# One down product moved ahead of an up product, and TensorE's expert loop turned by half a block

## The chip, the cores and the metric

The kernel runs on one core of a Trainium2 chip. TensorE multiplies, VectorE (DVE), ScalarE (ACT) and GpSimd (POOL) do the elementwise work and the indirect transfers, and SyncE (SP) issues the weight loads. The metric is the device time of one execution in microseconds (us). Times of trace rows are counted from the first instruction of the span.

## The reference, cut to what matters

One transformer block: attention, a residual, and then a mixture of experts. For each of 512 tokens a router picks 4 of 32 experts. Each expert is

```python
hu   = xb @ w1[e] + b1[e]                # "up": 1024 -> 2048
gate, lin = hu[:, :1024], hu[:, 1024:]
gate = min(gate, 7); lin = clip(lin, -7, 7)
act  = gate * sigmoid(1.702 * gate) * (lin + 1)
y    = act @ w2[e] + b2[e]               # "down": 1024 -> 1024
```

and the results, weighted by the gates, are added to the token's row. A final normalization follows. All weights are float32: 8 MB of w1 and 4 MB of w2 for each expert.

## The kernel before

The first part (attention, output projection, router, the tables of the routing) is not touched. The change is in the last part, which runs over blocks. A block is 32 tokens of one expert; an expert has as many blocks as its tokens need, and with this input there are 81 blocks (`nb`), numbered from 0. Experts stand in an order of places; place 0 has blocks 0, 1, 2, place 1 has blocks 3 and 4, place 2 starts with block 5.

**Weights.** The arena holds two experts, one for even places (`par` 0) and one for odd ones (`par` 1). SP loads one place after the other, w1 in four transfers of 2048 KB (L508) and w2 in two (L513), all on one queue. Quarter c of a new w1 waits on `w1_read`, until the first block of the place between has read its own quarter c; w2 waits until the last block that uses the old w2 has read it (`w2_read`, `y_done`).

**A block's work.** POOL gathers its token rows (`gather`, L600). DVE turns them into `xT` (`turn_rows`, L1255), the one buffer of its kind. TensorE does the up product into PSUM (`up`, L1816, 64 matmuls, and 4 for the bias, L1826). DVE and ACT make the activation (`hidden`, L1308 to L1314; `sigmoid`, L849), DVE turns it into `actT` (`turn_hidden`, L1301), also one buffer, and TensorE does the down product (`down`, L1854, 64 matmuls, 4 for the bias, L1846). DVE and ACT scale the result, and POOL adds it to the tokens' rows in memory (`scatter`, L609). A small product, `slot_product` (L1786), makes the list of tokens of a block some places ahead.

**Both places in code.** Which half of the arena a block reads is known only at run time. `up_of` (L1833) and `down_of` (L1862) are therefore an If and an Else, each with the whole product in it. `places_of` (L1802) loads a word of a table from SBUF into a register, and splits it into the places of two blocks.

**TensorE's order.** The first blocks are written out, the rest is a loop with two blocks to a pass. Before the change the order is

```
up0 up1 up2 down0 down1 up3 | slot5 down2 up4 | slot6 down3 up5 || slot7 down4 up6 | slot8 down5 up7 || ...
```

where `|` stands for the start of a block of the loop (test of `g < nb` or `g + 1 < nb`, L1894 and L1896, and the load of `places_of`) and `||` for the turn of the loop (L1892) as well. After the last block the loop runs on, with empty passes, up to its fixed count.

**DVE's order** in the written-out part is: rows of block 1 are turned inside `hidden(0)`, rows of block 2 inside `hidden(1)`, and so on, since `xT` is free only once the up product of the block before has ended.

Of the kernel before, what the change touches and what calls it, by code (L numbers as in the profile page):

```python
# [44 lines left out]
AHEAD = 64  # L45
MAXBLK = (T * TOPK + NE * (SLOTS - 1)) // SLOTS
NG = MAXBLK + 7
# [86 lines left out]
def build(nc, I, out):  # L134
    ctx = ExitStack()
    with ctx:
        def sb(name, shape, dt=F32):
            return ctx.enter_context(nc.sbuf_tensor("sb_" + name, shape, dt))
# [18 lines left out]
        def w1t(par):  # L157
            return arena[:, 3 * par * CH:(3 * par + 2) * CH].rearrange("p (k n) -> p k n", k=KT)
# [83 lines left out]
        def turned(o):  # L242
            return work[:, o:o + QD].rearrange("p (k s) -> p k s", k=KT)

        xg = [work[:, 0:QD], work[:, QD:2 * QD]]
        xT = turned(2 * QD)
        gat = [work[:, 3 * QD:4 * QD], work[:, 4 * QD:5 * QD]]
        actT = turned(5 * QD)
# [23 lines left out]
        prow = hot[0:1, 288:288 + NG]  # L272
# [27 lines left out]
        ptab = sb("ptab", [1, NG - 2], I32)  # L300
# [71 lines left out]
        EARLY = 8  # L372
        banks = [(2 * (u % 4), 2 * (u % 4) + 1) if g == 1 else (2 * (u % 4),)
                 for u, (g, _) in enumerate(units[:EARLY])]
        banks += [(3,), (4,), (5,), (3,), (4,)]
        banks += [(5,), (3, 4), (5,), (3,), (4, 5), (3,)] * 2 + [(4,)]
# [530 lines left out]
        def _(dve):  # L907
            step = Steps(dve, dve_step)
# [36 lines left out]
            for n, i in enumerate((1, 2, 3, 4, 0)):  # L945
                dve.wait_ge(tr_done, n + 1)
                s = 2 * (i % 4) if i else 2
                rows, c0 = (P, META + (i - 1) * P) if i else (META, 0)
# [275 lines left out]
            def slot_list(n):  # L1224

                e = dve.value_load(etab[0:1, n:n + 1] if isinstance(n, int) else etab[0:1, bass.ds(n, 1)],
                                   min_val=0, max_val=NE - 1)
                dve.wait_ge(list_done, n)
                slot_places(e, b64[:, bass.ds(n, 1)])
# [19 lines left out]
                nc.vector.tensor_tensor(sidx[:, bass.ds(n, 1)], c6[:, 6:7], c6[:, 8:9], ALU.subtract)\  # L1249
                    .then_inc(idx_kept, 1)  # L1250

            def turn_rows(b, r):

                dve.wait_ge(xg_in[b], r * 16 + 16)
                nc.vector.transpose(xT.rearrange("p (c j) s -> p c j s", j=2),  # L1255
                                    xg[b].rearrange("p (c q j) -> p c j q", c=Q, j=2)).then_inc(xT_ready, 1)

            dve.wait_ge(rank_done, 2)
# [22 lines left out]
            step(nc.vector.tensor_copy(prow, PS[0:1, 5, 0:NG]))  # L1281
            slot_list(1)
            turn_rows(0, 0)
            step(nc.vector.scalar_tensor_tensor(ptab[:, :], prow[:, 2:NG], float(AHEAD), prow[:, 0:NG - 2],
                                                ALU.mult, ALU.add))
            step(nc.vector.tensor_copy(order[:, :], PS[0:1, 4, NE:2 * NE]))
            step(nc.vector.tensor_copy(btabi[:, :], PS[0:1, 4, 0:NE]))
# [8 lines left out]
            def turn_hidden(n, b):  # L1296

                if not (isinstance(n, int) and n == 0):
                    dve.wait_ge(y_done, n)
                dve.wait_ge(act_ready, n + 1)  # L1300
                nc.vector.transpose(actT.rearrange("p (c j) s -> p c j s", j=4),  # L1301
                                    gat[b].rearrange("p (c q j) -> p c j q", c=2, j=4)).then_inc(actT_ready, 1)

            def hidden(n, b, r):

                gate, lin = PS[:, b, 0:QD], PS[:, b, QD:2 * QD]
                dve.wait_ge(up_done, n + 1)
                nc.vector.tensor_scalar(gat[b], gate, HID_LIMIT, None, ALU.min).then_inc(gat_ready, 1)  # L1308
                turn_rows(1 - b, r)
                nc.vector.tensor_scalar(lin, lin, HID_LIMIT, -HID_LIMIT, ALU.min, ALU.max).then_inc(hid_step, 1)  # L1310
                dve.wait_ge(sig_ready, n + 1)
                nc.vector.tensor_tensor(gat[b], gat[b], PS[:, 2 + b, 0:QD], ALU.mult).then_inc(hid_step, 1)
                dve.wait_ge(hid_step, 2 * n + 2)
                nc.vector.scalar_tensor_tensor(gat[b], lin, 1.0, gat[b], ALU.add, ALU.mult).then_inc(act_ready, 1)  # L1314
# [19 lines left out]
            nb = dve.value_load(btabi[0:1, NE - 1:NE], min_val=TOPK * T // SLOTS, max_val=MAXBLK)  # L1334
# [53 lines left out]
                                    egf[:, 2:3], None, ALU.is_equal).then_inc(sel2_ready, 1)  # L1388
            slot_rows(2, 0, 1)
            slot_list(3)  # L1390
            hidden(0, 0, 0)
            turn_hidden(0, 0)
            slot_rows(3, 1, 1)
            slot_list(4)
            hidden(1, 1, 1)
            slot_rows(4, 0, 2)
            slot_list(5)
            hidden(2, 0, 1)
            turn_hidden(1, 1)
            outputs(0, 0)  # L1400
# [21 lines left out]
            with dve.Fori(1, (MAXBLK + 1) // 2) as i:  # L1422
                g = 2 * i
# [9 lines left out]
        def _(pe):  # L1433
# [4 lines left out]
            for b in range(2):  # L1438
                mm(PS[0:HF, b, 0:328], rs[0:NE, 0:HF], hot[:, b * 328:(b + 1) * 328],
                   start=True, stop=True).then_inc(brow_mm, 1)  # L1440
            for i in (1, 2, 3, 4, 0):
                rows = META if i == 0 else P
# [5 lines left out]
                s = 2 * (i % 4) if i else 2  # L1448
# [242 lines left out]
            for i in range(HF * TT):  # L1691
# [3 lines left out]
                if i >= FILL:  # L1695
                    k = 2 * ((i - FILL) % 2)
# [86 lines left out]
            def slot_product(n):  # L1783
                pe.wait_ge(slots_ready, n * 5 + 5)
                for t in range(TT):
                    last = mm(PS[:, 5, 0:6], slots[:, t, :], g6c[:, t, :], start=t == 0, stop=t == TT - 1)  # L1786
                last.then_inc(list_done, 1)
# [12 lines left out]
            def places_of(n):  # L1800

                both = pe.value_load(ptab[0:1, n:n + 1] if isinstance(n, int) else ptab[0:1, bass.ds(n, 1)],  # L1802
                                     min_val=0, max_val=AHEAD * NE + NE)
                return both % AHEAD, both // AHEAD

            def group(c):
                return slice(c * SLOTS, (c + 1) * SLOTS)

            def up(g, at_place, par, b, s=None, listed=None):

                w = w1t(par).rearrange("p k (a c n) -> p k a c n", a=4, c=Q)
                for k in range(KT):
                    if k % 2 == 0:
                        pe.wait_ge(w1_full[par][k // 2], (at_place // 2) * 16 + 16)
                    for c in range(Q):
                        last = mm(PS[group(c), b, :].rearrange("p (a n) -> p a n", a=4),  # L1816
                                  xT[:, k, :], w[:, k, :, c, :], start=k == 0, stop=False)
                    if k % 2 == 1:
                        last.then_inc(w1_read, 1)
                    if k == 3 and listed is not None:  # L1820
                        slot_product(listed)
                if s is None:
                    pe.wait_ge(sel_ready, g + 1)
                bias1 = ball[:, 0:2 * D].rearrange("p (a c n) -> p a c n", a=4, c=Q)
                for c in range(Q):
                    last = mm(PS[group(c), b, :].rearrange("p (a n) -> p a n", a=4), selb[:, b if s is None else s, :],  # L1826
                              bias1[:, :, c, :], start=False, stop=True)
                last.then_inc(up_done, 1)

            def up_of(g, at_place, b, s=None, listed=None):  # L1830

                pe.wait_ge(xT_ready, g + 1)
                with pe.If(at_place % 2 == 0):  # L1833
                    up(g, at_place, 0, b, s, listed)
                with pe.Else():
                    up(g, at_place, 1, b, s, listed)
                pe.nop()

            def down(g, at_place, par, b):
# [20 lines left out]
            def down_of(g, at_place, b):  # L1860

                with pe.If(at_place % 2 == 0):  # L1862
                    down(g, at_place, 0, b)
                with pe.Else():
                    down(g, at_place, 1, b)
                pe.nop()
# [3 lines left out]
            up(0, 0, 0, 0, listed=2)  # L1870
            pe.wait_ge(tab_ready, 1)
            nb = pe.value_load(btabi[0:1, NE - 1:NE], min_val=TOPK * T // SLOTS, max_val=MAXBLK)
            second = places_of(0)[1]
            first, third = places_of(1)
            up_of(1, first, 1, listed=3)
            pe.wait_ge(sel2_ready, 1)
            pe.wait_ge(act_ready, 1)
            up_of(2, second, 0, 2, listed=4)
            down(0, 0, 0, 0)
            down_of(1, first, 1)  # L1880
            up_of(3, third, 1)

            def pe_block(g, b):

                here, following = places_of(g)
                slot_product(g + 3)
                down_of(g, here, b)
                with pe.If(g + 2 < nb):
                    up_of(g + 2, following, b)
                pe.nop()  # L1890

            with pe.Fori(1, (MAXBLK + 1) // 2) as i:  # L1892
                g = 2 * i
                with pe.If(g < nb):  # L1894
                    pe_block(g, 0)
                    with pe.If(g + 1 < nb):  # L1896
                        pe_block(g + 1, 1)
                    pe.nop()
                pe.nop()

# [2 lines left out]
            for t in range(TT):  # L1903
                for b in range(2):
                    for n in range(Q):
                        last = mm(PS[:, n + 4 * (t // 2), (t % 2) * QD:(t % 2 + 1) * QD],
                                  onehot[b][group(n), t * P:(t + 1) * P], gat[b][group(n), :],
                                  start=b == 0, stop=b == 1, skip_group_check=True)
# [30 lines left out]
```

## Time and profile before

| | us |
|---|---|
| median of 3 runs (1391.1 to 1392.87) | 1392.65 |
| the profiled execution's own time | 1391.69 |
| its span, first to last instruction | 1389.8 |
| PE busy | 1261.3 (91%) |
| DVE busy | 688.0 (49%) |
| up matmuls (L1816, x5184, 64 a block) | 599.1 |
| down matmuls (L1854, x5184) | 297.4 |
| chain that ended last | PE 73%, DMA 20%, DVE 4%, issue 2% |

The mean granted TensorE clock is 0.959 of full speed, and 440.13 MB are read from memory. "Busy" of PE counts matmuls from start to modelled end, and slow ones as well. A wait put down to "issue" is one in which the engine waited for nothing that the profile shows; what TensorE's sequencer did then (branches, register loads) can be asked for line by line. Those rows carry the name PEldq.

### The profile page before, as it was taken

To read this page: it belongs to the slowest core of one execution; us is meant where nothing else is said; L and a number is where in the kernel's file an instruction comes from. 1 tells how busy PE (TensorE), PEld (TensorE's weight loads), DVE (VectorE), ACT (ScalarE), POOL (GpSimd) and SP (SyncE) were. 2 spreads that over 40 slices of the span, in tenths; PEclk is the share of its full clock that TensorE was granted. 3 is DMA by queue.
4 is the path that set the end of the run, shared out by engine and by line. 5 is a ranking of instruction groups with operands and counts; after the bars stand their busy time and mean duration, and the time that the engine had idled before them with its cause. 6 is when DMAs were issued, how large, how long until landed. Compare 5 with 4: busy or idle time off the path is not lost.

```text
span 1389.8 us, 36015 instructions
## 1 busy us (share of the span) xinstructions
PE 1261.3 (91%) x13054; PEld 547.4 (39%) x13055; DVE 688.0 (49%) x2297; ACT 316.7 (23%) x575; POOL 298.4 (21%) x466
## 2 busy tenths in 40 slices
PE   7999999989589995999899989995999799989983
PEld 4656666555233331333233333331333233333332
DVE  2113333663735552565456645652656256645654
ACT  2012223433112220222122212220222022212212
POOL 5310000002212220222122312220222123312221
PEclk9999999999799997999999999997999899999996
DMA  9520002509778999999999999999999999999994
GB/s 327 148 58 1 1 0 86 222 23 383 306 301 359 417 417 425 417 419 418 417 419 417 419 417 375 403 419 422 416 419 418 422 416 421 416 418 419 417 420 168
DMA packets 51671, 458.87 MB, mean 330 GB/s; under 512 B 8629, under 2 KB 9013, under 8 KB 27061
## 3 DMA queue, kind: packets, MB, share of 16 engines
q1 hardware_dynamic: 43316, 436.38, 75.6%
q0 software_dynamic: 7936, 21.71, 5.9%
q8 instruction: 23, 0.38, 0.1%
q10 hardware_dynamic: 384, 0.32, 0.1%
q14 instruction: 12, 0.09, 0.0%
HBM read 440.13 MB, written 18.25 MB: 330 GB/s over the span
## 4 chain that ended last, share of the span: by engine, by line
PE 73%; DMA 20%; DVE 4%; issue 2%; ACT 1%; POOL 0%; DVEq 0%; ACTq 0%; SPq 0%; POOLq 0%
PE PS L1816 33%; DMA sb_arena<-in_w 19%; PE PS L1854 16%; PE PS L1489 4%; PE PS L1483 4%; PE PS L1486 2%; PE PS L1487 2%; PE PS L1683 2%; PE PS L1826 1%; PE PS L1846 1%; PE PS L1534 1%; DMA xfd<-sb_arena 1%; PE PS L1656 1%; PE PS L1786 1%; PE PS L1586 1%
## 5 line engine op out<-in xcount | busy, mean ns | idle before, releaser
L1816 PE MATMUL PS<-sb_arena,sb_work 128*32 128x512 f32 x5184 | 599.1, 612 | 67.8 <-DMA sb_arena<-in_w 61.7
L1816 PEld LDWEIGHTS PS<-sb_arena,sb_work 128*32 128x32 f32 x5184 | 158.1, 112 | 454.5 <-issue 355.7
L1854 PE MATMUL PS<-sb_arena,sb_work 128*32 128x256 f32 x5184 | 297.4, 382 | 3.6 <-issue 2.8
L1308 DVE TENSOR_SCALAR sb_work<-PS 128x256 f32<-128x256 f32 x81 | 34.4, 425 | 356.7 <-PE PS L1826 356.7
L1854 PEld LDWEIGHTS PS<-sb_arena,sb_work 128*32 128x32 f32 x5184 | 156.3, 111 | 114.4 <-issue 7.7
L849 ACT ACTIVATE PS<-sb_work 128x256 f32<-128x256 f32 x81 | 31.4, 388 | 518.8 <-DVE sb_work L1308 518.8
L857 ACT ACTIVATE sb_work<-PS,sb_gates 32x256 f32<-32x256 f32 x160 | 75.0, 469 | 257.8 <-PE PS L1854 252.6
L609 POOL DMA_INDIRECT accd<-sb_work,sb_sidc x79 | 113.6, 1438 | 33.4 <-issue 33.4
L617 POOL TENSOR_TENSOR sb_sm<-sb_sm 128x1 f32<-128x1 f32 x79 | 15.4, 195 | 489.0 <-DMA accd<-sb_work,sb_sidc 489.0
L888 ACT ACT_TABLE_LOAD x79 | 101.4, 1283 | 1.4
L1217 DVE TENSOR_SCALAR sb_slots<-sb_ca,sb_b,sb_rk 128x128 bf16<-128x128 f32 x332 | 92.6, 342 | 3.0 <-issue 3.0
L600 POOL DMA_INDIRECT sb_work<-xfd,sb_gidx x82 | 84.1, 1026 | 38.0 <-issue 36.1
L1301 DVE STREAM_TRANSPOSE sb_work<-sb_work 128x256 f32<-128x256 f32 x81 | 54.0, 667 | 59.2 <-PE PS L1854 59.1
L1330 DVE TENSOR_SCALAR sb_work<-PS,sb_gates 32x256 f32<-32x256 f32 x160 | 74.2, 464 | 3.9
L1483 PE MATMUL PS<-sb_arena 128*128 128x512 f32 x128 | 58.7, 600 | 1.2 <-DVE sb_arena L950 1.2
L1489 PE MATMUL PS<-sb_arena 128*128 128x512 f32 x128 | 58.6, 598 | 1.0 <-DVE sb_arena L972 1.0
L1003 DVE TENSOR_TENSOR_SCAN sb_arena<-sb_arena 128x1344 f32<-128x1344 f32 x8 | 23.7, 2957 | 70.2 <-ACT sb_arena L718 70.2
L1255 DVE STREAM_TRANSPOSE sb_work<-sb_work 128x256 f32<-128x256 f32 x82 | 36.1, 440 | 15.5 <-DMA sb_work<-xfd,sb_gidx 15.2
L599 POOL TENSOR_TENSOR sb_sm<-sb_sm 128x1 f32<-128x1 f32 x82 | 15.9, 194 | 128.8 <-DVE sb_gidx L1247 116.3
L1321 DVE TENSOR_SCALAR sb_work<-PS,sb_gates 128x256 f32<-128x256 f32 x79 | 38.2, 484 | 5.9 <-PE PS L1854 3.3
L1486 PE MATMUL PS<-sb_arena 128*128 128x264 f32 x128 | 39.3, 389 | 0.0
L1786 PEld LDWEIGHTS PS<-sb_g6c,sb_slots 128*128 128x128 bf16 x336 | 14.0, 97 | 63.2 <-issue 54.6
(274 smaller groups left out, 1166.4 us busy)
## 6 DMA issues: line engine op xcount, KB each, us to landing
sb_arena<-in_w SPq DMA_DIRECT2D x192, 2048.0 KB, 24.1
sb_arena<-in_w_in SPq DMA_DIRECT2D x6, 2048.0 KB, 20.7
sb_arena<-in_x SPq DMA_DIRECT2D x8, 512.0 KB, 8.2
sb_arena<-in_w_out SPq DMA_DIRECT2D x2, 2048.0 KB, 11.8
accd<-sb_arena SPq DMA_DIRECT2D x4, 512.0 KB, 9.2
xfd<-sb_arena SPq DMA_DIRECT2D x4, 512.0 KB, 6.5
sb_arena<-accd SPq DMA_DIRECT2D x4, 512.0 KB, 13.0
out<-sb_arena SPq DMA_DIRECT2D x4, 512.0 KB, 2.7
```

The costliest lines, as they stand in the source:

```text
L600: pool.indirect_dma_start(out=xg[b], out_offset=None, in_=xfd, in_offset=bass.IndirectOffsetOnAxis(ap=gidx[:, b:b + 1], axis=0)).then_inc( ...
L609: pool.indirect_dma_start(out=acc, out_offset=bass.IndirectOffsetOnAxis(ap=sidc[0:SLOTS, b:b + 1], axis=0), in_=yb[b], in_offset=None, com ...
L857: act.activation(yb[b][:, c * QD:(c + 1) * QD], PS[rows, 4 + 2 * b, 0:QD], ACT.Copy, scale=gates[rows, bass.ds(n, 1)]).then_inc(y_high, 1)
L888: act.preload_act_table(ACT.Sigmoid)
L1217: nc.vector.tensor_scalar(slots[:, t, :].rearrange("p (q s) -> p q s", s=SLOTS), ca[:, C_SLOT:C_SLOT + SLOTS].unsqueeze(1).to_broadcast([P ...
L1301: nc.vector.transpose(actT.rearrange("p (c j) s -> p c j s", j=4), gat[b].rearrange("p (c q j) -> p c j q", c=2, j=4)).then_inc(actT_ready, 1)
L1330: nc.vector.tensor_scalar(yb[b][:, c * QD:(c + 1) * QD], PS[rows, 4 + 2 * b, 0:QD], gates[rows, bass.ds(n, 1)], None, ALU.mult).then_inc(y ...
L1483: last = mm(PS[:, b, :], w[:, k, f * P:(f + 1) * P], nT[:, k, META:NKEY], **io)
L1486: mm(PS[:, b, 0:n], w[:, k, f * P:(f + 1) * P], nT[:, k, 0:n], **io)
L1489: last = mm(PS[:, b, :], nT[:, k, META + f * P:META + (f + 1) * P], w[:, k, :], **io)
L1816: last = mm(PS[group(c), b, :].rearrange("p (a n) -> p a n", a=4), xT[:, k, :], w[:, k, :, c, :], start=k == 0, stop=False)
L1854: last = mm(y[group(n), :], actT[:, k, :], w[:, k, n * QD:(n + 1) * QD], start=False, stop=k == KT - 1)
```

## The change

Three things. The order of TensorE becomes

```
up0 up1 up2 down0 down1 down2 up3 slot5 | up4 slot6 down3 | up5 slot7 down4 || up6 slot8 down5 | up7 slot9 down6 || ...
```

so that the third down product stands ahead of the fourth up product. A pass of the loop now begins with an up product, at block 3 instead of 2, and `places_of` gives the places of g and g + 1 instead of g and g + 2. The rows of block 1 are turned into `actT`, which no activation needs yet, instead of `xT`, and the rows of block 2 into `xT` right behind `hidden(0)`; `turn_hidden(0, 0)` moves behind `hidden(1, 1)`. DVE's, ACT's, POOL's and SP's loops stay as they are.

```diff
-            def turn_rows(b, r):
+            def turn_rows(b, r, rows=xT):
...
-            step(nc.vector.scalar_tensor_tensor(ptab[:, :], prow[:, 2:NG], float(AHEAD), prow[:, 0:NG - 2],
+            step(nc.vector.scalar_tensor_tensor(ptab[:, :], prow[:, 1:NG - 1], float(AHEAD), prow[:, 0:NG - 2],
...
-            def hidden(n, b, r):
+            def hidden(n, b, r=None):
...
-                turn_rows(1 - b, r)
+                if r is not None:
+                    turn_rows(1 - b, r)
...
-            hidden(0, 0, 0)
-            turn_hidden(0, 0)
+            turn_rows(1, 0, actT)
+            hidden(0, 0)
+            turn_rows(0, 1)
             slot_rows(3, 1, 1)
             slot_list(4)
-            hidden(1, 1, 1)
+            hidden(1, 1)
+            turn_hidden(0, 0)
...
-            second = places_of(0)[1]
-            first, third = places_of(1)
-            up_of(1, first, 1, listed=3)
+            first, second = places_of(1)
+            third = places_of(3)[0]
+            up_of(1, first, 1, listed=3, rows=actT)
             pe.wait_ge(sel2_ready, 1)
             pe.wait_ge(act_ready, 1)
             up_of(2, second, 0, 2, listed=4)
             down(0, 0, 0, 0)
             down_of(1, first, 1)
+            down_of(2, second, 0)
             up_of(3, third, 1)
+            slot_product(5)
 
             def pe_block(g, b):
 
                 here, following = places_of(g)
+                with pe.If(g + 1 < nb):
+                    up_of(g + 1, following, 1 - b)
+                pe.nop()
                 slot_product(g + 3)
                 down_of(g, here, b)
-                with pe.If(g + 2 < nb):
-                    up_of(g + 2, following, b)
-                pe.nop()
-
-            with pe.Fori(1, (MAXBLK + 1) // 2) as i:
-                g = 2 * i
+
+            with pe.Fori(1, MAXBLK // 2) as i:
+                g = 2 * i + 1
                 with pe.If(g < nb):
-                    pe_block(g, 0)
+                    pe_block(g, 1)
                     with pe.If(g + 1 < nb):
-                        pe_block(g + 1, 1)
+                        pe_block(g + 1, 0)
                     pe.nop()
                 pe.nop()
```

`up` and `up_of` get the same argument `rows=xT` and read `rows[:, k, :]`.

## Rows read from the trace of the kernel before

**Rows 1.** Chain that ended last, in order of time: start, length.

```profile
509.65 40.83 DMA sb_arena<-in_w
...
1314.51 34.82 DMA sb_arena<-in_w
```

**Rows 2.** DMA view, 850 to 1350 us: packets, MB, share of 16 engines.

```profile
q1 hardware_dynamic: 13571, 197.71, 92.7%
```

**Rows 3.** Timeline of SP's queue: start of the first issue, length of all.

```profile
392.15 5.80 SPq L508 DMA_DIRECT2D sb_arena<-in_w  x4
...
420.02 2.06 SPq L513 DMA_DIRECT2D sb_arena<-in_w  x2
...
460.72 5.49 SPq L508 DMA_DIRECT2D sb_arena<-in_w  x4
...
847.31 5.49 SPq L508 DMA_DIRECT2D sb_arena<-in_w  x4
...
880.16 5.47 SPq L508 DMA_DIRECT2D sb_arena<-in_w  x4
```

**Rows 4.** DMA view, 392.14 to 420.01 us, 40 slices of 0.70 us.

```profile
GB/s 0 329 71 282 423 376 376 447 423 470 412 400 417 453 435 423 376 423 423 447 423 470 400 341 288 400 423 476 470 400 376 423 206 159 35 0 0 24 0 0
```

**Rows 5.** DMA view, 392.14 to 460.71 us.

```profile
q1 hardware_dynamic: 1622, 23.69, 83.9%
```

**Rows 6.** DMA view, 800 to 860 us, 40 slices of 1.5 us.

```profile
GB/s 431 336 440 404 459 404 459 415 437 426 407 445 437 309 467 404 459 404 459 412 396 371 426 415 448 415 437 380 385 393 87 87 218 306 492 366 399 393 459 415
```

**Rows 7.** DMA view, 847.30 to 880.15 us.

```profile
q1 hardware_dynamic: 831, 12.30, 90.5%
```

**Rows 8.** DMA view, 847.30 to 1287.46 us.

```profile
q1 hardware_dynamic: 11915, 173.72, 92.8%
```

**Rows 9.** PE's timeline, first blocks: start, length, idle before and its releaser.

```profile
390.02 3.64 PE L1816 MATMUL PS<-sb_arena,sb_work 128*32 128x512 f32 x32 [1.40 <-DVE sb_work L1255]
...
402.06 3.66 PE L1854 MATMUL PS<-sb_arena,sb_work 128*32 128x256 f32 x64 [0.76 <-DVE sb_work L1301]
408.78 8.68 PE L1816 MATMUL PS<-sb_arena,sb_work 128*32 128x512 f32 x64 [3.06 <-issue]
...
433.72 2.96 PE L1854 MATMUL PS<-sb_arena,sb_work 128*32 128x256 f32 x49 [2.82 <-issue]
```

**Rows 10.** PE's timeline, a down and an up product later on.

```profile
841.75 3.63 PE L1854 MATMUL PS<-sb_arena,sb_work 128*32 128x256 f32 x64
845.21 7.04 PE L1816 MATMUL PS<-sb_arena,sb_work 128*32 128x512 f32 x64
```

**Rows 11.** TensorE's sequencer, 842.5 to 846 us, by line: ns min/median/max, first, last.

```profile
L1862 PEldq COMPARE_BRANCH  x1: 173/173/173, 843.9 to 843.9; - x1
...
L1814 PEldq FUSED_REGOPS  x1: 77/77/77, 844.6 to 844.6; - x1
```

**Rows 12.** The same, 838 to 842 us and 849 to 853 us.

```profile
L1896 PEldq ALU_OP  x1: 39/39/39, 839.0 to 839.0; - x1
...
L1802 PEldq SEQ_ASSERT  x1: 18/18/18, 839.9 to 839.9; - x1
...
L1892 PEldq ALU_OP  x1: 36/36/36, 849.9 to 849.9; - x1
...
L1802 PEldq SEQ_ASSERT  x1: 18/18/18, 851.3 to 851.3; - x1
```

**Rows 13.** The same for L1833 over the whole span.

```profile
L1833 PEldq COMPARE_BRANCH  x121: 66/177/3881, 380.6 to 1339.5; - x121
```

**Rows 14.** POOL's gathers (L600), 372 to 378 us, then the landings of 360 to 470.

```profile
L600 POOL DMA_INDIRECT sb_work<-xfd,sb_gidx x2: 971/984/997, 372.9 to 377.9; - x2
...
DMA to landing us min/median/max: 3.3/7.1/8.3
```

**Rows 15.** The end: PE's timeline, and the sequencer at L1896 from 1364 us.

```profile
1370.36 5.82 PE L1906 MATMUL PS<-sb_work,sb_arena 32*128 32x256 f32 x64 [4.68 <-issue]
...
L1896 PEldq COMPARE_BRANCH  x1: 218/218/218, 1364.5 to 1364.5; - x1
```

More of the change, by code:

```diff
@@ L1250, in slot_rows @@
                     .then_inc(idx_kept, 1)
-            def turn_rows(b, r):
+            def turn_rows(b, r, rows=xT):
                 dve.wait_ge(xg_in[b], r * 16 + 16)
-                nc.vector.transpose(xT.rearrange("p (c j) s -> p c j s", j=2),
+                nc.vector.transpose(rows.rearrange("p (c j) s -> p c j s", j=2),
                                     xg[b].rearrange("p (c q j) -> p c j q", c=Q, j=2)).then_inc(xT_ready, 1)
@@ L1807, in group, with up @@
                 return slice(c * SLOTS, (c + 1) * SLOTS)
-            def up(g, at_place, par, b, s=None, listed=None):
+            def up(g, at_place, par, b, s=None, listed=None, rows=xT):
                 w = w1t(par).rearrange("p k (a c n) -> p k a c n", a=4, c=Q)
@@ L1816, in up @@
                         last = mm(PS[group(c), b, :].rearrange("p (a n) -> p a n", a=4),
-                                  xT[:, k, :], w[:, k, :, c, :], start=k == 0, stop=False)
+                                  rows[:, k, :], w[:, k, :, c, :], start=k == 0, stop=False)
                     if k % 2 == 1:
@@ L1828, in up, with up_of @@
                 last.then_inc(up_done, 1)
-            def up_of(g, at_place, b, s=None, listed=None):
+            def up_of(g, at_place, b, s=None, listed=None, rows=xT):
                 pe.wait_ge(xT_ready, g + 1)
                 with pe.If(at_place % 2 == 0):
-                    up(g, at_place, 0, b, s, listed)
+                    up(g, at_place, 0, b, s, listed, rows)
                 with pe.Else():
-                    up(g, at_place, 1, b, s, listed)
+                    up(g, at_place, 1, b, s, listed, rows)
                 pe.nop()
```

## The prediction

> **What bounds the kernel now.** I read the chain that ended last first. From 509 us on it is made of TensorE's products with seven long waits for `sb_arena<-in_w` between them, 34.8 to 40.8 us each [rows 1]: TensorE runs two or three experts ahead of the stream of weights and then stands until it arrives. The DMA view says the same from the other side: from 850 to 1350 us the weight queue moves 197.71 MB in 500 us, 0.395 MB per us, with 92.7% of the engines' time [rows 2]; the rest goes to gathers and scatters. So the end is set by the stream. TensorE's time per block counts only where the stream has run dry and waits for TensorE to release a buffer. I looked for such places by comparing what SP has issued (2048 KB, 2.10 MB, a transfer) with what the queue has moved.
>
> There are four. (a) The loop's first load is issued at 392.15 [rows 3] into an idle queue; its bytes flow about 0.8 us later [rows 4]. (b) Those four transfers are 8.39 MB, 21.2 us of stream; with the slow, paced first slices they are through at 415.6, and the next issue is w2 at 420.02, released by down2, flowing at 420.8. That is a hole of 5.2 us [rows 3, 4]. (c) At 460.72, the w1 of place 4, 12 transfers (25.17 MB) have been issued and 23.69 moved [rows 5]: 1.48 MB, 3.8 us, are left, less 0.8 to start. The stream has 3.0 us to spare. (d) At 847.31 it is dry: two slices at 87 GB/s, gathers and scatters alone [rows 6]. At 880.16, six transfers later, 12.58 MB are issued and 12.30 moved [rows 7]: 0.3 MB left, 0.7 us, so nothing to spare. At the next thinnest, 1287.46, 84 transfers (176.16 MB) stand against 173.72 [rows 8]: 6.2 us, 5.4 to spare.
>
> **The change, part by part.**
>
> Block 1's rows in `actT`. The gather of block 1 is issued at 372.9; at the median of 7.1 us it lands at 380.0 [rows 14]. By then up0 has ended and xT is free in any case. The free buffer gains nothing for up1: 0. Block 2's rows can now be turned while up1 runs. Their gather is issued at 377.9, and even at 8.3 us, the longest of that stretch [rows 14], it lands at 386.2; with under half a microsecond for the transposition xT is ready at 386.7, and up1 ends at 390.02 - 1.40 = 388.6 [rows 9]. The wait of 1.40 us ahead of up2 [rows 9] goes: -1.4 us for TensorE, and for load (a), which up2's quarters release. What it costs: DVE now waits for this landing with `slot_rows(3)`, `slot_list(4)` and `hidden(1)` queued behind it, and they come some 2 us later. slot_list(4) is about 3 us of DVE work and so ready near 390; its reader sits in the middle of up2, at 388.6 + 3.6 = 392.2 [rows 9]. The activation of block 1 and gather 3 are needed only behind up2, after 396. If that cover were gone, up2 would stop in its middle for what is missing, 1 or 2 us.
>
> down2 ahead of up3. It needs `turn_hidden(2)`, which waits for down1 and takes 0.66 us, like the 0.76 us ahead of down1 [rows 9]: +0.8 us. It also brings w2's release from 420.0 to about 407, when place 2's w1 is still in flight: the hole of 5.2 us closes. With (a), the stream is up to 6.6 us earlier at 425.
>
> The half turn. From down3 on the order of products is unchanged, but the loop's bookkeeping moves. Before, `places_of` and the branches stood between an up product and the slot product. Up matmuls take 0.107 us each, and the sequencer runs far ahead there; the rows show no idle. Now they stand between a down and an up product. How far ahead is the sequencer there? At 843.9 it has dispatched the last matmul of down and begins the exit branch; TensorE starts the next up at 845.21 [rows 10, 11]: the lead is 1.3 us. In this time it now does 0.7 us (exit, tests, L1814, rows 11, to 844.7). The bookkeeping takes 839.0 to 840.0, 1.0 us, inside a pass, and 849.9 to 851.4, 1.5 us, at the turn [rows 12]. So 1.7 to 1.8 us against 1.3 inside a pass: 0.5 us of idle TensorE; 2.2 to 2.3 at the turn: 1.0 us. That is 1.5 us for two blocks, some 58 us over the 78 blocks left, and nearly all of it disappears in the seven waits of rows 1. It is paid only at (c) and (d).
>
> First pass through code. Two stops of TensorE carry no releaser: 3.06 and 2.82 us [rows 9]. The first is a branch of up_of that took 3.881 us [rows 13]; behind it up3 ran at a lower clock, 8.68 us against 7.04 [rows 9, 10], 1.64 more. Both are in code that runs for the first time; no such stop comes once the loop has gone round. From down0 to up5 seven products share 7.5 us, 1.1 each. The change makes one more product run on fresh code (the pair of bodies of down2 is written out, and then down3 and down4 come fresh as well). I take +1.1; the bounds are -7.5 (both stops fall away) and +5.5 (one more branch like the longest, 3.9, and the slow clock, 1.6). The Trainium skill, in "Runtime: NRT & Kernel Launch", section "Instruction fetch mechanics", says that fetch is sequential in blocks of 256 instructions and that a branch whose target has not been brought in must wait for a DMA; by it another If and Else speaks against the change. Its price is the branch's row; the sum would not move.
>
> **The sum.** TensorE's delay at (c), up7's first quarter: -1.4 + 0.8 + 1.1, and the idle ahead of up5, up6, up7: 0.5 + 1.0 + 0.5. That is +2.5. The stream had 3.0 to spare before; it is dry there now and starts again 2.5 - 3.0 = -0.5 us. So of the 6.6 us won at 425, 6.1 are lost again at 461. Then the wait at 509 sets TensorE by the stream again. From the restart at 805 to 847.31 there are four passages from down to up, two at a turn: 2 x 1.0 + 2 x 0.5 = +3.0, in full, since the stream is dry. To 880.16 three more, two at a turn: +2.5, nothing to spare. Elsewhere six passages cost at most 4.5, and 5.4 or more is to spare: 0. At the end TensorE's sequencer walks through the empty passes, 4.68 us ahead of L1906 [rows 15]; their number stays at seven, but the tests at L1888 and L1896 no longer stand behind the last down, 0.35 us each with their steps [rows 15]: -0.7. In all: -0.5 + 3.0 + 2.5 - 0.7 = +4.3 us. Against the profiled execution's 1391.69 that is 1396.0. It lies 0.96 below the median of the runs, so for a median I say 1392.65 + 4.3 = 1397.0.
>
> The weightiest figure is the lead of 1.3 us. The row gives it directly. The Trainium skill ("Advanced Engine Details and Errata", "Engine Queue Depths") gives TensorE a queue of 64 instructions. As 32 weight loads and 32 matmuls of 54 ns (3.46 us for 64 between the starts of rows 10) this would be a lead of 1.7 us. I take the row, since it is measured in this very passage.
>
> **The rivals.** They differ in k, the share of that idle time that shows. The sum is -3.2 + 7.5 k: 2.0 of the 7.5 at (c), 5.5 at (d).
>
> 1. The lead covers more. The mechanism: the sequencer is further ahead at the end of down than the start of its exit branch tells. At a lead 0.45 us longer, idle is 0.05 and 0.55: at (c) 0.65, at (d) 1.2 + 1.15. The sum is -0.2: 1392.5, no change. This is where the queue of 64 would put it. For it: TensorE's ends are modelled. Against it: its starts are not, and the lead is taken from starts. 12%.
> 2. The other side: the bookkeeping is hidden whole, k under 0.05, and the change does what it can at the front: 1389.4, faster. Place: the passage from down to up; price: 7.5 us less. Against it: 1.7 us of steps do not fit into 1.3. 10%.
> 3. More fresh-code stops: one more at 5.5 instead of 1.1, +8.7: 1401.4. 9%.
> 4. Fewer: both stops vanish. Then the stream keeps its 6.6 through (c), and -6.6 + 5.5 - 0.7 = -1.8: 1390.9. 5%.
> 5. The loop no longer stays in the instruction store, and each pass fetches: 1401 and far up. Its length is the same. 2%.
>
> My forecast has 62%. Its own range, with the idle at 20% more or less and the fresh code at 0 to 2.5, is 1394 to 1399.5.
>
> **Range and chances.** 1391.0 to 1400.8 takes in the forecast, rival 1 and most of the passage between, and leaves out rival 2 and the upper half of 3. A run can be told from no change from about 0.2%, 2.8 us. Slower by more is k above 0.8 with the rest as summed: three quarters of the forecast's 62%, 47%, and rivals 3 and 5, 11%: 58%. Faster: rival 2 and part of 4, 12%. The rest, 30%, is within.
>
> **What would show it.** In the trace after: no wait ahead of up2, and w2 of place 2 issued near 407 with no empty slices near 417; an idle time "issue" of 0.5 and 1.0 us in turn ahead of up products, which in the kernel before have none; the issues of 460.72 about 2.5 us later, and the hole before 847 grown by 3 us; a hole before 880, new. Wrong would be the forecast if TensorE shows no such idle, if the stops at first sight of code number none or three, or if the stream at 461 has not run dry.

## The result, and the profile after

The changed kernel takes 1406.31 us in the median of 4 runs (1402.58 to 1407.8), the kernel before 1392.76 beside it. The ratio is 1.0091, interval 1.0066 to 1.0115: slower by some 12.6 us. I had said slower, by 4.3, and 1391.0 to 1400.8. The direction was right, the size wrong by a factor of three, outside the range. The profiled execution took 1407.8 us, its span is 1406.0, 16.2 more than before. It was the slowest of the four, so what its trace adds up to lies some 3 us above the difference of the medians.

In the changed kernel's file the up matmul is L1819, the down matmul L1857, `places_of` L1805, and the branches of `up_of` and `down_of` L1836 and L1865.

What had been forecast for the passage from a down to an up product is there. The timeline of PE in the kernel after:

```profile
784.22 7.07 PE L1819 MATMUL PS<-sb_arena,sb_work 128*32 128x512 f32 x64 [0.51 <-issue]
...
796.50 7.07 PE L1819 MATMUL PS<-sb_arena,sb_work 128*32 128x512 f32 x64 [1.13 <-issue]
...
807.79 7.07 PE L1819 MATMUL PS<-sb_arena,sb_work 128*32 128x512 f32 x64
...
819.71 2.78 PE L1819 MATMUL PS<-sb_arena,sb_work 128*32 128x512 f32 x24 [0.77 <-issue]
```

Between the starts of these up products lie 12.28, 11.29 and 11.92 us; in the kernel before it is 10.95 wherever nothing waits. (Idle times under 0.15 us are not marked, so 807.79 carries none.) Over all passages of the loop without a wait for weights the mean is 11.79, 0.84 us a block more, where I had said 0.75. The sequencer, one passage of the kernel after:

```profile
L1865 PEldq COMPARE_BRANCH  x1: 169/169/169, 853.0 to 853.0; - x1
...
L1805 PEldq SEQ_ASSERT  x1: 18/18/18, 854.1 to 854.1; - x1
...
L1817 PEldq FUSED_REGOPS  x1: 77/77/77, 854.7 to 854.7; - x1
```

From 853.0, the start of the branch out of the down product, to 854.8 it is busy with branches and the load of `places_of`, 1.8 us, against a lead of 1.3: the time by which the sequencer is ahead of the multiplying array there.

The surprise is in the waits. These are TensorE's waits, first in the kernel before, then in the kernel after, for 480 to 690, 690 to 940 and 940 to 1360 us (total, times, longest):

```profile
PE PS L1816 <- DMA sb_arena<-in_w: 21.4, 7, 10.3
...
PE PS L1816 <- DMA sb_arena<-in_w: 4.9, 2, 3.9
...
PE PS L1816 <- DMA sb_arena<-in_w: 35.5, 11, 9.7
```

```profile
PE PS L1819 <- issue: 10.0, 15, 1.1
PE PS L1819 <- DMA sb_arena<-in_w: 8.8, 4, 3.1
...
PE PS L1819 <- issue: 14.1, 20, 1.1
...
PE PS L1819 <- issue: 18.4, 26, 1.1
PE PS L1819 <- DMA sb_arena<-in_w: 15.6, 7, 4.1
```

Before, TensorE stood still for weights for 62 us in all, and for 4.9 us only between 690 and 940. Between 560 and 690 the kernel before has 6.2 us of such waiting:

```profile
PE PS L1816 <- DMA sb_arena<-in_w: 6.2, 2, 3.9
```

In [rows 1] I had read pieces of 35 to 41 us as such waits. They are not: a piece of that chain goes back from the landing of a transfer to its issue, and most of that time TensorE was at work on blocks it already had. In the kernel after, no wait for weights is left between 560 and 940. TensorE does not catch up there, and carries its lateness into the thin places, the loads for which the stream has little or no time to spare.

The issues of loads of the kernel after, on SP's queue:

```profile
387.70 5.80 SPq L508 DMA_DIRECT2D sb_arena<-in_w  x4
...
407.95 2.69 SPq L513 DMA_DIRECT2D sb_arena<-in_w  x2
...
464.30 5.49 SPq L508 DMA_DIRECT2D sb_arena<-in_w  x4
...
751.43 5.47 SPq L508 DMA_DIRECT2D sb_arena<-in_w  x4
...
856.96 5.49 SPq L508 DMA_DIRECT2D sb_arena<-in_w  x4
...
893.03 5.47 SPq L508 DMA_DIRECT2D sb_arena<-in_w  x4
```

Beside [rows 3]: w2 is issued at 408 instead of 420, as forecast. Then 460.72 has become 464.30, 847.31 has become 856.96 and 880.16 has become 893.03. The DMA view of the kernel after, 735 to 765 us (slices of 0.75 us), 830 to 890 (1.5 us) and 850 to 910 (1.5 us):

```profile
GB/s 415 481 459 393 393 502 437 421 426 421 393 415 371 344 399 415 481 459 393 393 388 159 0 350 87 284 371 481 268 382 421 371 546 481 350 371 524 437 415 437
...
GB/s 415 459 415 423 451 339 371 513 360 492 371 418 270 0 0 0 0 87 175 164 448 352 369 481 382 470 393 415 437 358 472 404 426 448 385 434 470 298 467 404
...
GB/s 0 0 0 33 55 197 317 371 380 396 470 404 459 401 440 388 399 382 470 393 470 399 431 393 399 431 426 11 87 186 306 388 385 418 437 437 426 391 472 366
```

The hole ahead of 857 is now four empty slices and three thin ones, where [rows 6] had two at 87. There is a hole at 891, which was forecast, and one at 751, which was not.

### The profile page after: what moved, and what is told of

Same layout as the page of the kernel before. It is cut to its first block, busy times and chain, and to the rows that moved or that the text cites. A ratio compares the mean times of both kernels' runs of the same rounds, so it can differ in the third digit from the quotient of the medians.

```text
span 1406.0 us, 36000 instructions
## 1 busy us (share of the span) xinstructions
PE 1268.4 (90%) x13054; PEld 558.3 (40%) x13055; DVE 683.4 (49%) x2297; ACT 316.6 (23%) x575; POOL 298.5 (21%) x466
## 4 chain that ended last, share of the span: by engine, by line
PE 81%; DMA 9%; issue 5%; DVE 4%; ACT 1%; POOL 0%; DVEq 0%; ACTq 0%; POOLq 0%; SPq 0%
PE PS L1819 38%; PE PS L1857 19%; DMA sb_arena<-in_w 7%; PE PS L1492 4%; PE PS L1486 4%; PE PS L1489 2%; PE PS L1490 2%; PE PS L1686 2%; PE PS L1849 1%; PE PS L1829 1%; PE PS L1789 1%; PE PS L1537 1%; PE PS L1659 1%; PE PS L1589 1%; PE PS L1513 1%
## 5 line engine op out<-in xcount | busy, mean ns | idle before, releaser
L1819 PE MATMUL PS<-sb_arena,sb_work 128*32 128x512 f32 x5184 | 589.6, 606 | 74.6 <-issue 46.0
L1819 PEld LDWEIGHTS PS<-sb_arena,sb_work 128*32 128x32 f32 x5184 | 166.3, 111 | 459.2 <-issue 419.9
L1857 PE MATMUL PS<-sb_arena,sb_work 128*32 128x256 f32 x5184 | 302.3, 386 | 4.3 <-issue 2.8
L1857 PEld LDWEIGHTS PS<-sb_arena,sb_work 128*32 128x32 f32 x5184 | 158.2, 112 | 118.6 <-issue 13.5
L600 POOL DMA_INDIRECT sb_work<-xfd,sb_gidx x82 | 84.4, 1029 | 27.6 <-issue 22.4
L1489 PE MATMUL PS<-sb_arena 128*128 128x264 f32 x128 | 39.3, 389 | 0.0
L1490 PE MATMUL PS<-sb_arena 128*128 128x264 f32 x128 | 39.0, 386 | 0.0
```

The costliest lines, as they stand in the source:

```text
L600: pool.indirect_dma_start(out=xg[b], out_offset=None, in_=xfd, in_offset=bass.IndirectOffsetOnAxis(ap=gidx[:, b:b + 1], axis=0)).then_inc( ...
L1489: mm(PS[:, b, 0:n], w[:, k, f * P:(f + 1) * P], nT[:, k, 0:n], **io)
L1490: last = mm(PS[:, b + 1, 0:n], w[:, k, f * P:(f + 1) * P], nT[:, k, n:NKEY], **io)
L1857: last = mm(y[group(n), :], actT[:, k, :], w[:, k, n * QD:(n + 1) * QD], start=False, stop=k == KT - 1)
```

## The experiments

All ran beside the kernel before on the same chip. Ratios are to it, with 95% intervals.

**e1, the half turn alone.** The order of products is that of the kernel before.

```diff
             up_of(3, third, 1)
+            slot_product(5)
+            down_of(2, second, 0)
...
-                slot_product(g + 3)
-                down_of(g, here, b)
-                with pe.If(g + 2 < nb):
-                    up_of(g + 2, following, b)
+                with pe.If(g + 1 < nb):
+                    up_of(g + 1, following, 1 - b)
+                pe.nop()
+                slot_product(g + 3)
+                down_of(g, here, b)
...
-            with pe.Fori(1, (MAXBLK + 1) // 2) as i:
-                g = 2 * i
+            with pe.Fori(1, MAXBLK // 2) as i:
+                g = 2 * i + 1
```

> The kernel before with the half turn alone: the loop begins with an up product and the loads of places_of stand between a down and an up product, while the order of all products, and DVE's order, are those of before. Theory A (the idle time ahead of up products is the loss): idle of 0.5 and 1.1 us ahead of up products in turn, as in the changed kernel, and 1402 to 1408 us, some +12. Theory B (the order at the front, with up4 waiting for its rows and the code that runs for the first time, is the loss): within 2 us of the kernel before, whatever the idle time per block.

Measured: 1.0083 (1.0060 to 1.0106), 1405.3 us. The half turn alone is as slow as the whole change, and its profile waits 24.4 us for weights between 480 and 1360, as the changed kernel's does. Theory B falls.

**e2, the order alone.** The changed kernel with `up_of(4, fourth, 0)` written out and the loop in its old form, starting at block 3.

```diff
...
+            fourth = places_of(2)[1]
...
             up_of(3, third, 1)
             slot_product(5)
+            up_of(4, fourth, 0)
...
-                with pe.If(g + 1 < nb):
-                    up_of(g + 1, following, 1 - b)
-                pe.nop()
                 slot_product(g + 3)
                 down_of(g, here, b)
+                with pe.If(g + 2 < nb):
+                    up_of(g + 2, following, b)
+                pe.nop()
```

> The changed kernel with its loop turned back: down2 ahead of up3 and the early rows stay, up4 is written out too, and the bookkeeping stands behind an up product again, with nothing idle ahead of the next one. Theory A: no idle ahead of up products in the loop, and 1389 to 1394 us, near the kernel before: the loss is gone. Theory B: still some 1400 us or more.

Measured: 1.0011 (0.9997 to 1.0024), 1394.7 us. The loss is gone, and so is every idle time "issue" ahead of up products in the loop:

```profile
PE PS L1819 <- DMA sb_arena<-in_w: 59.2, 19, 9.5
```

That line is its only wait ahead of an up product between 480 and 1360 us. The front itself gains nothing.

**e3 and e7, the early rows alone**, twice the same kernel: the kernel before with DVE's part of the change and `rows=actT` for up1.

```diff
-            hidden(0, 0, 0)
-            turn_hidden(0, 0)
+            turn_rows(1, 0, actT)
+            hidden(0, 0)
+            turn_rows(0, 1)
...
-            hidden(1, 1, 1)
+            hidden(1, 1)
+            turn_hidden(0, 0)
...
-            up_of(1, first, 1, listed=3)
+            up_of(1, first, 1, listed=3, rows=actT)
```

> The kernel before with only the rows of block 1 in the down operand's buffer and those of block 2 turned early. Both theories: the wait of 1.40 us ahead of up2 goes, the stream of weights starts 1.4 us earlier and stays so to the end: -1.4 us, 1391.3, hardly told from no change. If the end does not follow the stream's start: 0.

> The kernel of e3 once more, word for word: the kernel before with only the early rows. If its gain is real, again 1 to 4 us below the kernel before, and the two together exclude no change.

Measured: 0.9986 (0.9973 to 0.9998), 1390.3 us, and 0.9990 (0.9970 to 1.0009), 1390.9 us. The second run alone does not exclude no change. Weighted together, taken as independent, they give 0.9987 (0.9977 to 0.9998). This part of the change is worth 1.8 us by that (0.3 to 3.2), and is the one version found that beats both kernels. Up2 follows up1 with no wait in its profile, as in the changed kernel's.

**e4 and e5, the suspected cost dosed.** The kernel before with two loads, then with one, between down and up.

```diff
+                for _ in range(2):
+                    places_of(g)
                 with pe.If(g + 2 < nb):
                     up_of(g + 2, following, b)
```

> The kernel before with two more loads of places_of between the down and the up product of every block of the loop (1.6 us of sequencer steps, 0.6 used before, a lead of 1.3: 0.9 to 1.0 us idle ahead of each up product, as much as the changed kernel has at its worse passage). Nothing in the order changes. Theory A: +12 us or more, 1405 to 1412, since the mean idle time is somewhat above that of the changed kernel. Theory B: within 2 us of the kernel before.

> The kernel before with one more load of places_of between down and up in every block (0.8 us of steps, 0.1 to 0.5 us idle ahead of an up product, some 0.3 in the mean). Theory A, first form (the waits for weights swallow all idle time but that ahead of the thin places): idle ahead of up7, the four passages before the issue of 847 and the three before 880 show, 0.3 x 7 or 8, +2 to +2.5 us. Theory A, second form (the waits are short, about 5 us in the cycle that ends at 805, and what exceeds them is carried into the next thin place): 12 blocks x 0.3 = 3.6 us is still less than 5, so also +2 to +2.5. Both say 1395 to 1396; if even one load costs 8 or more, the size of the waits is not what decides.

Measured: two loads 1.0149 (1.0127 to 1.0171), 1415.4 us; one load 1.0015 (0.9998 to 1.0032), 1395.7 us. The period of a block, where nothing waits, is 11.88 us and 11.23, against 10.95. So loads at the wrong place, with nothing else touched, give the whole effect, and it is not proportional: 0.28 us a block cost about 2 us (by the interval 0 to 4.5), 0.93 cost 22.

**e6, half of the idle time taken away from the changed kernel.** The load for the second block of a pass is made behind the first up product.

```diff
...
-                here, following = places_of(g)
+                here, following = places
                 with pe.If(g + 1 < nb):
                     up_of(g + 1, following, 1 - b)
                 pe.nop()
+                nxt = places_of(g + 1) if ahead else None
                 slot_product(g + 3)
                 down_of(g, here, b)
+                return nxt
...
-                    pe_block(g, 1)
+                    nxt = pe_block(g, 1, places_of(g), True)
                     with pe.If(g + 1 < nb):
-                        pe_block(g + 1, 0)
+                        pe_block(g + 1, 0, nxt)
```

> The changed kernel, with the load for the second block of a pass moved up behind the up product of the first, where it is hidden. Idle stays ahead of one up product in two, about 1.1 us: 0.55 in the mean where the changed kernel has 0.84. First form: in proportion to the idle at the thin places, 2/3 of the loss of 12.6: 1401. Second form: 12 blocks x 0.55 = 6.6 us just exceeds the 5 us of waiting before 805, so less than in proportion is carried over: 1397 to 1400.

Measured: 1.0000 (0.9983 to 1.0018), 1394.7 us. Its timeline shows the idle at every second passage alone:

```profile
794.76 7.07 PE L1819 MATMUL PS<-sb_arena,sb_work 128*32 128x512 f32 x64 [1.12 <-issue]
805.74 7.04 PE L1819 MATMUL PS<-sb_arena,sb_work 128*32 128x512 f32 x64
817.62 7.07 PE L1819 MATMUL PS<-sb_arena,sb_work 128*32 128x512 f32 x64 [0.76 <-issue]
828.60 7.04 PE L1819 MATMUL PS<-sb_arena,sb_work 128*32 128x512 f32 x64
```

The loss is gone with 0.59 us a block still there (period 11.54). Both forms of my theory had said more (1397 to 1401). With e5 and e4 this reads as a threshold: 0.28 and 0.59 us a block cost 2 and 0 us, with intervals up to 4.5 and 2.5, while 0.84 costs 12 and 0.93 costs 22.

**e8 and e9, the same cost at two places.** The two loads of e4 only for blocks below 42, or only from 46 on.

```diff
+                with pe.If(g < 42):          # e9: g >= 46
+                    for _ in range(2):
+                        places_of(g)
+                pe.nop()
                 with pe.If(g + 2 < nb):
```

> As e4, but the two extra loads run only for blocks below 42, that is ahead of up4 to up43, which takes in the thin places before 847 and 880; a test and a branch (0.2 us, still within the lead) stand in every block. If idle time costs by its place: the whole of what e4 loses up to there, 14 to 16 us: 1406 to 1410. If it costs by its sum: 40 of 77 passages, half of e4's 22: 1404.

> The same loads only for blocks from 46 on, ahead of up48 to up80, where TensorE waits for weights at 954, 976, 1079, 1102, 1231 and 1349 us and the stream has 5.4 us or more to spare. By place: 33 passages of some 1.0 us against waits of 10 to 20 us in most of the cycles, so only what the last two cycles cannot swallow, +3 to +6: 1396 to 1400. By the sum: 33 of 77, +9.5: 1403.

Measured: early 1.0137 (1.0111 to 1.0162), 1411.2 us; late 1.0069 (1.0053 to 1.0084), 1403.2 us. By the sum, the expectations had said 1404 and 1403; by the place, 1406 to 1410 and 1396 to 1400. So neither form holds for both: early costs 7 us more than the sum says, and late costs what the sum says and twice what I had said by the place. Place matters, +18 for 40 passages against +10 for 33, with 1.08 and 1.03 us of idle time in each. The two add up to more than e4's 22, in which a passage has 0.93.

Early: in its profiled execution the issue that stands at 880.16 in the kernel before comes at 896.25, 16.1 us later, and the whole span is 17.0 us longer. TensorE still waits for weights in the products that start at 1226 and 1353. What is lost by 893 stays, and no more is lost after it. The late kernel's DMA view, 1280 to 1340 us, shows where a part of its loss arises:

```profile
GB/s 393 470 404 418 445 437 339 448 393 330 63 164 208 437 350 404 426 437 437 396 434 426 344 464 415 448 426 410 442 426 311 464 404 459 404 434 451 426 355 399
```

Its stream runs dry at 1295, ahead of the load that was the next thinnest place before [rows 8]. The 5.4 us to spare there had been set against six passages. But in e9 the late idle had also used up the waits that the kernel before has at 1216 and 1222 (no wait for weights ahead of an up product between 1103 and the end), so some sixteen passages bore on it. The balance of that stretch fits: TensorE is 0.6 us late at 1103, 21 passages at 1.03 are 21.6 us, and the kernel before has 8.9 us of waiting there and 2.4 in products at the lower clock. That leaves 10.9, and the last down product comes 10.25 later. Another 1.0 us stands between it and the final product.

## Why the prediction was wrong, step by step

**The step that failed:** "That is 1.5 us for two blocks, some 58 us over the 78 blocks left, and nearly all of it disappears in the seven waits of rows 1. It is paid only at (c) and (d)." The waits are not 35 us each, they are 62 us of standing still in all, unevenly spread, and a little more in products that then run at a lower clock (3.5 us in the two products with waits between 560 and 812; the granted clock is 0.84 in the mean of 671 to 682). Against them stand some 64 us of new idle time, 76 passages at 0.84. Where a cycle has less waiting than new idle, TensorE comes out late, and the next thin place bears the lateness too. The 4.9 us between 690 and 940 are such a cycle: eleven blocks at 0.84 make 9.2 us. I had let TensorE be set by the stream at 805 and counted four passages to 847; in the trace after it is not set by the stream anywhere between 560 and 940.

The sum of that stretch closes. From the last stop for weights at 551 to the issue of 857 there are 26 passages, 21.8 us of new idle time, and the product at 551 ran 1.7 us longer at the lower clock. The kernel before has 6.2 + 4.9 = 11.1 us of waiting there and the 3.5 us of slow products. What is left over is 8.9, and the weights at 551 had landed 0.9 later: 9.8 us, and the issue came 9.65 later. It also gives an estimate of the threshold: 11.1 + 3.5 us over 26 passages is 0.56 us a block, between the 0.28 of e5 and the 0.84 of the change, and next to the 0.59 of e6.

How the profiled execution's loss builds up, by the moments at which the stream is dry (the stream's lateness is then that of the issue) and by the start of the final product. Up0 starts at 369.37 in the one execution and at 366.93 in the other, in code that the change leaves alone, so some 2.4 us of such a difference lie between the executions:

| to | stream or TensorE late by | step | forecast |
|---|---|---|---|
| 464, (c) | 3.58 - 3.0 to spare = +0.6 | +0.6 | -0.5 |
| 857, (d) | +9.65 | +9.0 | +3.0 |
| 893, (d) | +12.87 | +3.2 | +2.5 |
| final product | 1385.99 - 1370.36 = +15.6 | +2.8 | -0.7 |

About 2 of the 9.0 fall at 751, where the stream has run dry as well. The last step: before, the last up product waited for its weights; now TensorE is behind the stream, and nothing waits (kernel after, PE's timeline):

```profile
1360.67 7.07 PE L1819 MATMUL PS<-sb_arena,sb_work 128*32 128x512 f32 x64 [1.13 <-issue]
...
1385.99 6.67 PE L1911 MATMUL PS<-sb_work,sb_arena 32*128 32x256 f32 x64 [3.47 <-issue]
```

e6 supports the account from the other side: with 0.59 us a block, the loss goes. Its profiled execution, the slowest of its twelve, shows no wait between 564 and 961 either. Its issue that belongs to 464 came 8.1 us later than before, 5.1 beyond the 3.0 to spare, and the one that belongs to 857 came 6.5 later: the stretch between added 1.3. No run stands between 0.59 and 0.84, so the threshold is an estimate and not measured.

**Right.** The mechanism and its place: the lead of 1.3 us, the steps of 1.7 and 2.3 us, idle of 0.5 and 1.0 us (in the mean 0.56 and 1.16 measured, 0.84 a block where 0.75 was said). e1, e2 and e4 show it by experiment. Rival 1, the longer lead, falls: idle would have been 0.3 a block. It is where the queue of 64 instructions would put it that the Trainium skill gives in "Advanced Engine Details and Errata", "Engine Queue Depths"; the trace shows a lead of 1.27 us here, not the 1.7 estimated from it. Rival 2 falls with it. Rival 4 falls, since no stop vanished, and so does rival 5: the DMA view of the kernel after shows no instruction fetch between 470 and 1340 us. The wait ahead of up2 is gone, its worth at the front is borne out by e3 and e7. w2's early issue and the closing of the hole at 417 came as said (a shorter one opens at 422), and the gain was lost again by 464, as said. The 0.7 us at the end are there too: from the start of the last down product to the final product 9.87 us instead of 10.60, hidden under the lateness.

**A term left out.** Ahead of up4 stands a wait that I did not see. In the old order down2 lay between up3 and up4 and hid the turning of block 4's rows; now up4 follows up3 and the slot product at once:

```profile
378.16 3.64 PE L1819 MATMUL PS<-sb_arena,sb_work 128*32 128x512 f32 x32 [1.43 <-DVE sb_work L1255]
...
404.85 5.30 PE L1857 MATMUL PS<-sb_arena,sb_work 128*32 128x256 f32 x58 [2.09 <-issue]
411.15 7.07 PE L1819 MATMUL PS<-sb_arena,sb_work 128*32 128x512 f32 x64 [1.00 <-issue]
...
420.07 7.07 PE L1819 MATMUL PS<-sb_arena,sb_work 128*32 128x512 f32 x64 [1.44 <-DVE sb_work L1255]
...
444.03 0.40 PE L1849 MATMUL PS<-sb_ball,sb_selb 128*32 128x256 bf16 x4 [4.08 <-issue]
444.21 6.44 PE L1857 MATMUL PS<-sb_arena,sb_work 128*32 128x256 f32 x64
```

**Fresh code** was sized too low. The rows show stops of 2.09, 1.00, 0.73 (at 429.79) and 4.08 us, four where the prediction had named three as a sign against it, and two down products at the lower clock, 5.30 for 58 matmuls and 6.44 for 64 where 3.6 is usual (granted clock 0.66 from 405 to 410 and 0.51 from 444.3 to 450), against 5.88 and 1.64 before. That is some 5 us more, where I had said 1.1. So rival 3 came near in its term (5.5), but not in its price of 8.7: the stream started again at (c) only 0.6 us late, and in e2, which has such stops too, the whole costs 0.1%. The stop of 4.08 is the longest of these branches, 5.8 us in `down_of`, ahead of down4, the first one to take that way:

```profile
L1865 PEldq COMPARE_BRANCH  x1: 5802/5802/5802, 438.1 to 438.1; - x1
```

From up1 to the issue at (c) TensorE lost 6.4 us (3.58, and 2.84 by which up1 started earlier, in code that the change does not touch), where I had said 2.5. e2 has both costs of the new order and no half turn; against e3, in the same session, it is slower by 0.25% of the time, some 3.5 us by the ratios, so down2 ahead of up3 gives nothing back. Which of the two costs weighs more was not separated.

## What to carry to other kernels

Before you hide a cost in a wait, read the wait where the engine stands idle (the view of waits, stretch by stretch), not in the chain, whose DMA pieces run from issue to landing. Then balance each stretch between two thin places: new idle time against waiting in that stretch, and what is left over goes into the next. And put a loop's register loads and branches behind the instructions that keep the queue full for longest: here the sequencer has 2.4 us behind matmuls of 512 columns (it begins the branch out of the up product at 849.7, and the products behind it start at 852.08), behind those of 256 only 1.3. These are the rows of the kernel before:

```profile
L1833 PEldq COMPARE_BRANCH  x1: 177/177/177, 849.7 to 849.7; - x1
...
852.08 0.39 PE L1826 MATMUL PS<-sb_ball,sb_selb 128*32 128x512 bf16 x4
```

## What the runs showed of the hardware

The lead of TensorE's sequencer is 1.27 to 1.28 us at the end of a down product, in 37 of the 38 passages of the kernel before in which the trace has the branch out of that product (1.31 in the other). That is the time of 24 matmuls at 54 ns. A register load with its arithmetic takes the sequencer 0.65 us where two stand in a row, in e4 from 844.8 to 845.5, and 0.3 of it is the load itself:

```profile
L1802 PEldq TENSOR_LOAD <-sb_ptab x2: 305/305/305, 844.8 to 845.5; - x2
```

The same 0.65 lies between the periods of e5 and e4, 0.28 and 0.93 us a block above 10.95. A branch into code that had not run yet took 2.9 and 5.8 us in the kernel after and 3.9 in the kernel before, and some 0.2 later on. And idle time of TensorE cost nothing that could be told at 0.59 us a block and 12 to 22 us at 0.84 and 0.93, depending on how much waiting each stretch still had.
